# A two-block transformer kernel: first attention normalised on GpSimd, packed gate unit, bias and fill banks reassigned

## Chip, cores and metric

The kernel runs on one core of a Trainium2 chip, as one program. The metric is the device time of one execution in microseconds (us). Engines are named as in the profile: PE is TensorE's matmul side, PEld its weight loads, DVE is VectorE, ACT ScalarE, POOL GpSimd, SP SyncE.

## What is computed

A sequence of 512 tokens with 1024 features goes through two blocks.

- Block one: RMS norm, one wide projection, then three kinds of attention over 8 query heads in 2 groups (compressed keys, selected key blocks, window), each multiplied by a sigmoid gate and added up; beside it a convolution branch (31 taps, 512 channels). With 512 tokens, 8 selection blocks and 16 to be chosen, the selection takes every block, and the window of 512 takes every earlier key. Then a merge, an output projection and a convolutional feed-forward net of width 2816.
- Block two: an even layer with a dense grouped attention and a latent attention (8 heads each, 512 keys), an odd layer with windowed attention of 16 heads with a sink, and a last RMS norm.

The part that the change touches most, from the reference:

```python
p_s = jax.nn.softmax(jnp.where(dist_s >= 0, s_s, NEG_INF), axis=-1)
o_s = jnp.einsum('bgjtm,bgtmd->btgjd', p_s.astype(vsg.dtype), vsg)
...
p_w = jax.nn.softmax(jnp.where(valid_w, s_w, NEG_INF), axis=-1)
o_w = jnp.einsum('bgjts,bsgd->btgjd', p_w.astype(vw.dtype), vw)
...
g = jax.nn.sigmoid(gate_logits).reshape(b, s, G, J, 3)
o = g[..., 0:1] * o_c + g[..., 1:2] * o_s + g[..., 2:3] * o_w
```

## The kernel before

Everything is kept transposed, features on the 128 partitions and 512 tokens along the free dimension. The weights come as 171 units of 128 output features by 1024 input features, in the fixed order of UNITS. SP loads a unit into one of five raw buffers as soon as the PE has finished the unit five places earlier (`unit_done`). POOL splits it: `whi` is the weight rounded to fp32r (L1076, L1077), `wlo` the rest (two halves, L1071); `w_hi` counts units whose first part is made, `w_split` finished ones. The input is split in the same way, so that a unit on the PE (`unit`, L478) is 8 chunks of three 128x512 matmuls: high by high, low by high, high by low; the matmuls of a unit accumulate in one PSUM bank. Each engine's program is written out by hand; where attention steps and units share the PE, the loops below interleave them.

**Banks.** There are eight PSUM banks of 128x512. `Banks.take(pe, pool, key)` gives the next bank of a pool (a tuple of bank numbers) in turn, and makes the PE wait until the last user of that bank was read (`freed`). Turns are counted by the tuple, so that two pools written as the same tuple share a turn: EOUT_REST, E_BANKS and O_BANKS are all (3, 0, 1, 2). TR, for sums and spreads, is (4, 5).

**First attention ("N", L576 to L621).** 32 steps, 4 head pairs by 2 branches (selected, window) by 4 query tiles; step s has qt+1 key tiles. In iteration i the PE does `n_scores(i)` (L585), `n_turn(i-2)` (the probabilities turned, L595), two chunks of a gate unit `ga` or `gb` (L478) and `n_values(i-3)` (L607). DVE adds the bias and takes the maximum (`n_max`, L1958), ACT does the exponential with its row sum (L1329) and copies the turned tile (L1338). The probabilities are not normalised: for each pair p of head and branch DVE takes the reciprocal of 8 row sums and multiplies by the gate (L1967, L1969), the PE spreads the result over the partitions (`n_spread`, L619, 16 rows of the trace), ACT copies that (L1346), DVE multiplies the values bank by it (L1976), adds the branches (L1980) and the compressed branch (L1984). Between these, DVE works through 75 of the convolution's taps (L1832, one 128x512 multiply-add each, both inputs in SBUF), a number per iteration by TAPS_AT. POOL only splits weights in this stage.

**Raw units ("e" and "o", `raw_units`).** The first three units of block two's layers use the input before its norm. The DVE scales their banks afterwards and adds a correction, a 128x2 matmul pair per chunk (`bias`, L495), summed in banks of its own: BIAS_BANK, here bank 3 for the first two units and bank 4 for the third. Of the layer "e", `spread("e")` (L566) lies in bank 4 as well, and is read until the last of eight `h_split` multiplications (L1749), which make the normed input for the fourth unit, `ekr`. In layer "o" the fourth unit `oq3` takes its bank from O_BANKS; `low` (L2407) frees the banks of the raw units oq0, oq1, oq2 one after another once the input is normed.

**Second attention ("AB").** 32 steps; iteration i: scores (L879, L886), turn (L900), `key_prep` (L925, banks C_R), `ab_values(i-3)` (L913), `query_prep` (L930), half a gate unit in bank 0. DVE frees the banks of the preparations. POOL normalises these probabilities (`normalize`: a power -1 of two row sums, L1111, and one multiplication for each half, L1115). **Third attention ("C")**: the same with windows; its values (L1020) always accumulate in bank 6, which `c_out` (L2446) frees after `gates`.

**Start.** Four `conv` units run on unnormed input, high parts first (L658, a wait for `w_split`), then the low parts (L666).

**Gates.** Unit ("tok", 2) has 24 used output rows, the gate logits; it is turned by four transposes.

Of the kernel before, what the change touches and what calls it, by code (L numbers as in the profile page):

```python
# [21 lines left out]
P = 128  # L22
T = 512
# [68 lines left out]
OOUT_BANKS, OOUT_REST = (0, 3, 7), (1, 2, 0, 3)  # L92
# [27 lines left out]
RAW_BANKS, BIAS_BANK = (0, 1, 2), ((3,), (4,))  # L120
# [70 lines left out]
AB_FILL_BANK, AB_S, AB_O = (0,), (1, 2), (3, 6)  # L191
C_FILL, C_S, C_T, C_O, C_R = (3, 0), (1, 2), (4, 5), (6,), (7,)


def program(nc, d, out, known):
    found = {}
    ctx = ExitStack()
    with ctx:
# [80 lines left out]
        nspread = area(T)  # L279
# [94 lines left out]
        def pt_c(p, half, kt, at, n):  # L374

            start = ((p % 2 * 2 + half) * TT + kt) * 3 * P + at * P
            return pt3[:, start:start + n * P]
        sel2, minus1 = sb("sel2", [2]), sb("minus1", [2])
        table = sb("table", [2 * len(ROOTS)])
# [74 lines left out]
        def _(pe):  # L454
# [34 lines left out]
            def bias(tag, layer, j, k, s):  # L489

                if k == 0:
                    bank.take(pe, BIAS_BANK[j // 2], (tag, "bias", j))
                b = bank.tiles[BIAS_BANK[j // 2][0]]
# [5 lines left out]
            def raw_units(tag, layer, units, src, sums_, spread_):  # L499
# [14 lines left out]
                unit(*units[2], src=src, pool=RAW_BANKS, extra=lambda k, s: bias(tag, layer, 2, k, s))  # L514

# [83 lines left out]
            def n_values(s):  # L599
                i, br, qt = n_steps[s]  # L600
                pe.wait_ge(*ptc.at(("N", s, 1)))
                if qt == 0:
                    bank.take(pe, N_O, ("O", "N", s // TT))
                b = bank.tiles[found[("bank", ("O", "N", s // TT))]]
                for kt in range(qt + 1):
                    for half in range(2):
                        m = mm(b[64 * half:64 * half + 64, qt * P:(qt + 1) * P],  # L607
                               vtok[:, kt, br * P + half * HD:br * P + half * HD + HD],
                               npt[:, s % 2, half, kt * P:(kt + 1) * P], start=(kt == 0), stop=(kt == qt),
                               skip_group_check=True)  # L610
                m.then_inc(*pv_done.up(("N", s)))

            def n_spread(p):
                pe.wait_ge(*dve_did.at(("N", "rinv", p)))
                b = bank.take(pe, C_R, ("N", "R", p))
                for qt in range(TT):
                    for half in range(2):
                        x = n_col(p, half, qt)
                        m = mm(b[64 * half:64 * half + 64, qt * P:(qt + 1) * P],  # L619
                               rinv[:, x:x + 1].to_broadcast([P, HD]), ident[:, :], start=True, stop=True)  # L620
                m.then_inc(*pe_did.up(("N", "R", p)))  # L621
# [28 lines left out]
            for i in range(CONV_FIRST):  # L650
                u = UNIT[("conv", i)]
                pe.wait_ge(w_split.sem, u + 1)
                b = bank.take(pe, CONV_BANKS, ("conv", i))
                for k in range(DC):
                    if i == 0:
                        pe.wait_ge(*act_did.at(("n1", "rhi", k)))
                    for w in (whi, wlo):
                        mm(b[:, :], w[:, u % WS, k * P:(k + 1) * P], raw_n(k)[0],  # L658
                           start=(k == 0 and w is whi), stop=False)
# [37 lines left out]
            for i in range(3):  # L697
                unit("tok", i)
# [4 lines left out]
            for i in range(4):  # L703
                unit("q", i, pool=Q_BANKS)
                if i == 0:
                    turn_unit("tok", 2, tokbuf(2))
# [3 lines left out]
            for i in range(n + 4):  # L710
# [14 lines left out]
                if i >= 6 and (i - 6) % TT == 0:  # L725
                    n_spread((i - 6) // TT)
# [136 lines left out]
            unit("ega", 1, pool=E_BANKS)  # L863
            unit("ega", 2, pool=E_BANKS)
# [58 lines left out]
            def key_prep(j):  # L923
                b = bank.take(pe, C_R, ("KN", j))
# [16 lines left out]
            for i in range(n + 4):  # L941
# [8 lines left out]
                if 3 <= i < n + 3:  # L950
                    ab_values(i - 3)
# [4 lines left out]
                if i < 2 * len(AB_FILL):  # L956
                    if i % 2 == 0:
                        part = unit(*AB_FILL[i // 2], inline=False, pool=AB_FILL_BANK)
                    for k in range(4):
                        part(i % 2 * 4 + k)  # L960
                for j, k0, k1 in EOUT_FIRST.get(i, ()):
# [42 lines left out]
            def c_values(i):  # L1004
# [9 lines left out]
                b = bank.tiles[C_O[0]]  # L1014
# [40 lines left out]
        def _(pool):  # L1055
# [10 lines left out]
                            pattern=[[-1, P]], channel_multiplier=1).then_inc(*pool_did.up("const"))  # L1066

# [40 lines left out]
            def normalize(name, s, x, probs):  # L1108
# [1496 lines left out]
```

## Time and profile before

| | |
|---|---|
| runs, us | 1337.38, 1344.39, 1339.45; median 1339.45 |
| profiled execution, us | 1342.96; its span 1341.2 |
| mean granted TensorE clock | 0.982 |
| busy in the span | PE 1298.4, PEld 1027.0, DVE 782.6, ACT 445.6, POOL 818.2 |

Busy time is the union of an engine's instructions. Matmuls overlap in the pipeline: a 128x512 matmul lasts 0.39 in its row, but one starts every 0.23, so time on the PE is read from starts, or from the chain of waits, where a piece is as long as it moves the chain on. An interval after an instruction, in square brackets, is idle time before it and what ended it.

### The profile page before, as it was taken

The page shows a single profiled execution, that of the slowest core. Times are in us where ns is not written, and L with a number is a line of the kernel's source. Part 1 is how long each engine was busy: PE and PEld are TensorE (multiplying, and loading weights), DVE is VectorE, ACT ScalarE, POOL GpSimd, SP SyncE. Part 2 cuts the span into 40 slices and gives each one's busy share as a digit, 9 for nine tenths or more (in the row PEclk, how much of TensorE's full clock was granted, in tenths as well). Part 3 has the DMA queues.
Part 4 walks back from the last instruction along what each step waited for, and adds up shares of the span by engine and source line. Part 5 has one row for each costly group of instructions (what it writes and reads, how often), then busy time and mean ns, then how long its engine had stood idle before and what let it go on. Part 6 is the DMA issues. An engine that isn't in the chain of part 4 may idle for free.

```text
span 1341.2 us, 19796 instructions
## 1 busy us (share of the span) xinstructions
PE 1298.4 (97%) x7118; PEld 1027.0 (77%) x7118; DVE 782.6 (58%) x1512; ACT 445.6 (33%) x947; POOL 818.2 (61%) x916
## 2 busy tenths in 40 slices
PE   7999999999999999999999979999999998999996
PEld 5898767788888888888888868877567786866675
DVE  4897888914654777777652455463655362055532
ACT  5201556513121211222110341245767331145521
POOL 5885322446676766667697463665745464678842
PEclk9999999989999999999999979999999998999998
DMA  4622111122353455555653123221000221311111
GB/s 177 233 80 79 32 40 41 33 64 82 100 180 112 164 199 198 190 188 190 203 171 95 50 91 134 79 64 48 1 1 1 79 85 63 95 47 49 32 48 63
DMA packets 37524, 130.21 MB, mean 97 GB/s; under 512 B 4544, under 2 KB 4928, under 8 KB 37184
## 3 DMA queue, kind: packets, MB, share of 16 engines
q1 hardware_dynamic: 26640, 93.07, 22.0%
q10 hardware_dynamic: 10800, 35.98, 7.2%
q8 instruction: 57, 0.93, 0.3%
q14 instruction: 27, 0.22, 0.1%
HBM read 126.94 MB, written 2.10 MB: 96 GB/s over the span
## 4 chain that ended last, share of the span: by engine, by line
PE 89%; issue 4%; POOL 4%; DVE 1%; ACT 1%; DMA 0%; POOLq 0%; DVEq 0%; ACTq 0%; SPq 0%
PE bank L478 52%; PE bank L777 9%; PE bank L755 3%; POOL wlo L1071 3%; PE bank L913 2%; PE bank L900 2%; PE bank L607 2%; PE bank L585 2%; PE bank L595 2%; PE bank L1020 2%; PE bank L990 2%; PE bank L658 1%; PE bank L886 1%; PE bank L891 1%; PE bank L681 1%
## 5 line engine op out<-in xcount | busy, mean ns | idle before, releaser
L1071 POOL TENSOR_TENSOR wlo<-raw,whi 128x512 fp32r<-128x512 f32 x342 | 466.8, 1385 | 31.1 <-ACT whi L1612 18.1
L478 PE MATMUL bank<-ysplit,whi 128*128 128x512 f32 x984 | 315.5, 399 | 0.2 <-DVE xbuf L2388 0.2
L1076 POOL TENSOR_TENSOR whi<-raw,ones 128x2 fp32r<-128x2 f32 x155 | 40.5, 261 | 373.4 <-DMA raw<-in_w 373.0
L478 PE MATMUL bank<-hhi,whi 128*128 128x512 f32 x536 | 219.8, 410 | 6.1 <-issue 5.5
L478 PEld LDWEIGHTS bank<-ysplit,whi 128*128 128x128 f32 x984 | 183.9, 190 | 39.0 <-issue 3.9
L478 PE MATMUL bank<-hhi,wlo 128*128 128x512 f32 x536 | 211.2, 394 | 0.0
L478 PE MATMUL bank<-hlo,whi 128*128 128x512 f32 x536 | 210.9, 393 | 0.0
L478 PE MATMUL bank<-ysplit,wlo 128*128 128x512 f32 x496 | 194.7, 393 | 0.0
L1077 POOL TENSOR_SCALAR whi<-raw 128x1022 fp32r<-128x1022 f32 x155 | 170.8, 1102 | 0.0
L478 PEld LDWEIGHTS bank<-hhi,whi 128*128 128x128 f32 x536 | 102.1, 190 | 31.8 <-issue 12.3
L478 PEld LDWEIGHTS bank<-hhi,wlo 128*128 128x128 f32 x536 | 101.8, 190 | 22.5
L478 PEld LDWEIGHTS bank<-hlo,whi 128*128 128x128 f32 x536 | 102.2, 191 | 18.4
L478 PEld LDWEIGHTS bank<-ysplit,wlo 128*128 128x128 f32 x496 | 94.1, 190 | 20.1
L1832 DVE SCALAR_TENSOR_TENSOR arena<-first,arena 128x512 f32<-128x512 f32 x120 | 106.6, 938 | 0.2
L1111 POOL TENSOR_TENSOR rinv<-rsum,minus 128x2 f32<-128x2 f32 x64 | 46.2, 722 | 86.2 <-ACT arena L1551 66.8
L1437 ACT ACTIVATE arena<-bank,cols 128x512 f32<-128x512 f32 x44 | 34.4, 781 | 177.7 <-DVE bank L2153 177.7
L1115 POOL TENSOR_SCALAR arena<-arena,rinv 128x512 f32<-128x512 f32 (+2 forms) x128 | 78.1, 624 | 6.3
L2315 DVE CUSTOM_DVE_ANT_0 arena<-bank,arena 128x512 f32<-128x512 f32 x64 | 44.2, 690 | 53.4 <-PE bank L891 34.0
L777 PE MATMUL bank<-hhi,whi 128*128 128x512 f32 x176 | 68.5, 389 | 0.0
L777 PE MATMUL bank<-hlo,whi 128*128 128x512 f32 x176 | 68.5, 389 | 0.0
L777 PE MATMUL bank<-hhi,wlo 128*128 128x512 f32 x176 | 68.5, 389 | 0.0
L2153 DVE TENSOR_TENSOR bank<-bank,arena 128x512 f32<-128x512 f32 x44 | 30.7, 698 | 50.4 <-PE bank L478 50.4
(318 smaller groups left out, 2156.2 us busy)
## 6 DMA issues: line engine op xcount, KB each, us to landing
raw<-in_w SPq DMA_DIRECT2D x171, 512.0 KB, 3.6
arena<-in_ada ACTq DMA_DIRECT2D x48, 512.0 KB, 4.3
xbuf<-in_xT ACTq DMA_DIRECT2D x12, 256.0 KB, 5.2
xbuf<-in_w ACTq DMA_DIRECT2D x1, 2048.0 KB, 10.7
first<-in_w ACTq DMA_DIRECT2D x1, 2048.0 KB, 8.9
out_t<-xbuf SPq DMA_DIRECT2D x8, 256.0 KB, 2.3
xbuf<-in_xT SPq DMA_DIRECT2D x4, 256.0 KB, 6.6
first<-in_uq ACTq DMA_DIRECT2D x1, 768.0 KB, 6.9
```

The source lines that it names most:

```text
L478: m = mm(b[:, :], w[:, s, k * P:(k + 1) * P], x, start=(k == 0 and part == 0), stop=(k == DC - 1 and part == 2))
L755: m = mm(b[:, :], w[:, u % WS, kk * P:(kk + 1) * P], x, start=(k == 0 and part == 0), stop=(k == 3 and part == 2))
L777: m = mm(b[:, :], w[:, u % WS, n * P:(n + 1) * P], x, start=(i == 0 and part == 0), stop=(i == FC - 1 and part == 2))
L1071: return g.tensor_tensor(wlo[:, s, at], raw[:, s, at], whi[:, s, at].bitcast(F32), ALU.subtract)
L1076: g.tensor_tensor(whi[:, s, 0:2], raw[:, s, 0:2], ones[:, :], ALU.mult)
L1077: g.tensor_scalar(whi[:, s, 2:D], raw[:, s, 2:D], 1.0, 1.0, ALU.mult, ALU.mult)\
L1111: g.tensor_tensor(rinv[:, x:x + 2], rsum[:, x:x + 2], minus1[:, :], ALU.pow)\
L1115: g.tensor_scalar(probs(half), probs(half), rinv[:, x + half:x + half + 1], 1.0, ALU.mult, ALU.mult)\
L1437: A(ua[:, i % 4, :], bank.of(("up", i))[:, :], ACT.Identity, scale=col("ffw", order_up(i) * 3 + 2), bias=col("ffb", order_up(i)))\
L1832: V.scalar_tensor_tensor(cacc[:, c, :], z[:, c, k:k + T], w, cacc[:, c, :], ALU.mult, ALU.add)\
L2153: V.tensor_tensor(b[:, :], b[:, :], spread2, ALU.mult).then_inc(*dve_did.up(("un", i)))
L2315: link(V.tensor_tensor_reduce(abp[:, s % 3, half, :], bank.of(("S", "AB", s, half))[:, :], zero, 1.0, -3.0e38, ALU.add, ALU.max, nmax[:, x ...
```

## The change

1. `gate_unit` replaces the unit ("tok", 2): POOL copies the 24 low columns beside the 24 high ones (`whi` columns 32 to 55), so that two matmuls per chunk do for three; `turn_gates` adds the two groups by a matmul with `sum24`.
2. The first attention's probabilities are normalised and gated on POOL (`n_norm`); the PE's `n_turn` waits for that. `n_spread`, its copy and DVE's part go. Both branches of a head pair accumulate in one bank, and `n_out` is one addition. POOL's splits in the stage are cut in three parts, between the normalisations.
3. The first `conv` unit starts when `whi` is there, and does all its high weights first. ACT runs a small Copy before its first real one.
4. BIAS_BANK is bank 3 alone; the third unit's bias goes into the bank of the layer's sums ("fe", "sum") or ("o", "sum"), read and freed earlier.
5. ega1 and ega2 take banks 0 and 3 by pools of their own; fills and preparations of the second attention take banks 0 and 7 in turn, and stand ahead of `ab_values`. E_BANKS' turn is two shorter, so that oq3 falls on bank 0 and not on 2.
6. The third attention's values alternate between banks 6 and 7, OOUT_BANKS ends in 6, and `c_out` stands ahead of `gates`.

```diff
-OOUT_BANKS, OOUT_REST = (0, 3, 7), (1, 2, 0, 3)
+OOUT_BANKS, OOUT_REST = (0, 3, 6), (1, 2, 0, 3)
-RAW_BANKS, BIAS_BANK = (0, 1, 2), ((3,), (4,))
+RAW_BANKS, BIAS_BANK, SUM_OF = (0, 1, 2), (3,), {"e": "fe", "o": "o"}
-AB_FILL_BANK, AB_S, AB_O = (0,), (1, 2), (3, 6)
-C_FILL, C_S, C_T, C_O, C_R = (3, 0), (1, 2), (4, 5), (6,), (7,)
+AB_FILL_BANK, AB_S, AB_O = (0, 7), (1, 2), (3, 6)
+C_FILL, C_S, C_T, C_O, C_R = (3, 0), (1, 2), (4, 5), (6, 7), (7,)
...
                 if k == 0:
-                    bank.take(pe, BIAS_BANK[j // 2], (tag, "bias", j))
+                    pool = BIAS_BANK if j < 2 else (found[("bank", (SUM_OF[tag], "sum"))],)
+                    bank.take(pe, pool, (tag, "bias", j))
...
+            def gate_unit():
+                u = UNIT[("tok", 2)]
+                pe.wait_ge(w_split.sem, u + 1)
+                b = bank.take(pe, WIDE, ("tok", 2))
+                for k in range(DC):
+                    for part, x in enumerate(h_parts(k)):
+                        m = mm(b[:, :], whi[:, u % WS, k * P:(k + 1) * P], x,
+                               start=(k == 0 and part == 0), stop=(k == DC - 1 and part == 1))
+                m.then_inc(*unit_done.up(u))
...
                 for half in range(2):
-                    pe.wait_ge(*p_ready.at(("N", s, half)))
+                    pe.wait_ge(*p_norm.at(("N", s, half)))
...
-                if i >= 6 and (i - 6) % TT == 0:
-                    n_spread((i - 6) // TT)
...
-            unit("ega", 1, pool=E_BANKS)
-            unit("ega", 2, pool=E_BANKS)
+            unit("ega", 1, pool=AB_FILL_BANK[:1])
+            unit("ega", 2, pool=AB_O[:1])
...
-                b = bank.take(pe, C_R, ("KN", j))
+                b = bank.take(pe, AB_FILL_BANK, ("KN", j))
...
+            def n_norm(s):
+                i, b, qt = n_steps[s]
+                normalize("N", s, n_col(s // TT, 0, qt), lambda half: np_[:, s % 3, half, 0:(qt + 1) * P],
+                          lambda half: gate3[:, qt, 3 * (i + 4 * half) + 1 + b:3 * (i + 4 * half) + 2 + b])
...
+            for i in range(len(n_steps)):
+                n_norm(i)
+                if i % TT:
+                    split_part(first + i // TT, i % TT - 1)
...
+            def n_out(i):
+                dve.wait_ge(*act_did.at(("cmp", "o", i)))
+                dve.wait_ge(*pv_done.at(("N", 8 * i + 7)))
+                V.tensor_tensor(nacc(i), bank.of(("O", "N", i))[:, :], ncmp(i), ALU.add)\
+                    .then_inc(*dve_did.up(("N", "o", i)))
```

How the order changes, at two places. On the PE in the first attention, end of iteration 6 and start of iteration 7, before (L607 values, L619 the spread, L585 scores, L595 the turn, L638 and L630 turn and scores of the compressed branch):

```order
L607 MATMUL bank<-arena 64x128 x8
L619 MATMUL bank<-ident,rinv 64x128 x8
L585 MATMUL bank<-split_r 128x512 x6
L595 MATMUL bank<-ident,arena 128x128 x4
L638 MATMUL bank<-ident,arena 128x128 x2
L630 MATMUL bank<-split_r 128x64 x12
```

The same place now (the functions stand on other lines: L628 values, L606 scores, L616 the turn, L649 and L641 the compressed branch):

```order
L628 MATMUL bank<-arena 64x128 x8
L606 MATMUL bank<-split_r 128x512 x6
L616 MATMUL bank<-ident,arena 128x128 x4
L649 MATMUL bank<-ident,arena 128x128 x2
L641 MATMUL bank<-split_r 128x64 x12
```

The spread is gone from the PE, and nothing stands in its place. On POOL, the first two steps and a half of that attention now (before, only rows like the first three stand here, one group per unit; L1130 is the power, L1134 the multiplications, L1119, L1120 and L1090 the parts of a split):

```order
L1095 TENSOR_TENSOR whi<-raw,ones 128x2
L1096 TENSOR_SCALAR whi<-raw 128x1022
L1090 TENSOR_TENSOR wlo<-raw,whi 128x512 x2
L1130 TENSOR_TENSOR rinv<-rsum,minus 128x2
L1134 TENSOR_SCALAR arena<-arena,rinv 128x128 x2
L1130 TENSOR_TENSOR rinv<-rsum,minus 128x2
L1134 TENSOR_SCALAR arena<-arena,rinv 128x256 x2
L1119 TENSOR_TENSOR whi<-raw,ones 128x2
L1120 TENSOR_SCALAR whi<-raw 128x1022
L1130 TENSOR_TENSOR rinv<-rsum,minus 128x2
L1134 TENSOR_SCALAR arena<-arena,rinv 128x384 x2
L1090 TENSOR_TENSOR wlo<-raw,whi 128x512
```

Each step now has a power and two multiplications on POOL, and a unit's split is spread over three steps.

## Rows read from the trace of the kernel before

**Rows 1.** Waits of the PE, whole span: releaser, us in total, times, longest.

```profile
PE bank L658 <- POOL wlo L1071: 9.7, 1, 9.7
PE bank L495 <- DVE bank L1749: 8.4, 1, 8.4
PE bank L478 <- issue: 5.5, 1, 5.5
...
PE bank L1020 <- DVE arena L2446: 1.4, 1, 1.4
```

**Rows 2.** Timeline around the raw units of layer e: start, us, instruction, idle before.

```profile
785.18 0.17 DVE L1692 SCALAR_TENSOR_TENSOR stat<-bank,stat 128x8 f32<-128x8 f32 x1
...
795.84 0.39 PE L478 MATMUL bank<-ysplit,wlo 128*128 128x512 f32 x1
...
804.53 1.60 DVE L1760 SCALAR_TENSOR_TENSOR hlo<-bank,modc,hhi 128x512 fp32r<-128x512 f32 x2
...
804.67 0.37 PE L495 MATMUL bank<-shr,whi 128*128 128x2 f32 x1 [8.45 <-DVE bank L1749]
...
813.51 0.48 PE L478 MATMUL bank<-hhi,whi 128*128 128x512 f32 x1
```

**Rows 3.** Chain of waits in the same unit, one chunk: start, length, what.

```profile
810.79 0.12 PE bank L495 x2
810.90 0.80 PE bank L478 x3
```

**Rows 4.** Busy by window: PE, PEld, DVE, ACT, POOL, granted clock, DMA.

```profile
804.67:809.48 4.81, 4.80 (x15) 4.09 (x16) 1.35 (x2) 0.67 (x1) 0.00 (x0) 0.51 0.00 0
```

**Rows 5.** Timeline, DVE, before the fourth unit of layer o.

```profile
1112.09 2.09 DVE L2407 SCALAR_TENSOR_TENSOR ysplit<-bank,cols,ysplit 128x512 fp32r<-128x512 f32 x3
```

**Rows 6.** Groups with shapes apart, 149 to 271: busy us, mean ns.

```profile
L1832 DVE SCALAR_TENSOR_TENSOR arena<-first,arena 128x512 f32<-128x512 f32 x75 | 64.0, 901 | 0.0
...
L619 PE MATMUL bank<-ident,rinv 128*64 128x128 f32 x128 | 8.3, 273 | 0.0
...
L1976 DVE TENSOR_TENSOR first<-bank,arena 128x512 f32<-128x512 f32 x4 | 2.7, 682 | 0.0
```

**Rows 7.** Busy by window, first attention: all of it, then its later part.

```profile
135.45:261.90 126.45, 124.81 (x997) 91.53 (x996) 112.62 (x263) 74.54 (x220) 40.83 (x34) 1.00 0.11 35
...
217.03:261.90 44.87, 44.87 (x380) 33.52 (x378) 44.13 (x95) 28.04 (x84) 15.59 (x12) 1.00 0.12 37
```

**Rows 8.** Taps while POOL is idle, groups of DVE in 175.5 to 186.5.

```profile
L1832 DVE SCALAR_TENSOR_TENSOR arena<-first,arena 128x512 f32<-128x512 f32 x9 | 6.3, 745 | 0.0
```

**Rows 9.** Timeline: a split's high part amid taps.

```profile
151.79 1.56 POOL L1077 TENSOR_SCALAR whi<-raw 128x1022 fp32r<-128x1022 f32 x1
```

**Rows 10.** POOL's groups, whole span, with shapes apart.

```profile
L1077 POOL TENSOR_SCALAR whi<-raw 128x1022 fp32r<-128x1022 f32 x155 | 170.8, 1102 | 0.0
L1111 POOL TENSOR_TENSOR rinv<-rsum,minus 128x2 f32<-128x2 f32 x64 | 46.2, 722 | 86.2 <-ACT arena L1551 66.8 <-ACT arena L1644 19.3
L1115 POOL TENSOR_SCALAR arena<-arena,rinv 128x512 f32<-128x512 f32 x64 | 44.7, 713 | 3.2
...
L1115 POOL TENSOR_SCALAR arena<-arena,rinv 128x256 f32<-128x256 f32 x32 | 15.0, 482 | 1.6
```

**Rows 11.** Timeline, step 22: the exponential's end and the turn that follows it.

```profile
228.63 0.18 ACT L1329 ACTIVATION_READ_ACCUMULATOR arena<-arena,nmax 128x1 f32 x1
...
232.18 0.87 PE L595 MATMUL bank<-ident,arena 128*128 128x128 f32 x6
```

**Rows 12.** Timeline, start: the fourth unit's split, and the low parts' first matmul.

```profile
20.27 2.57 POOL L1071 TENSOR_TENSOR wlo<-raw,whi 128x512 fp32r<-128x512 f32 x2
...
26.68 1.07 PE L666 MATMUL bank<-split_r,whi 128*128 128x512 f32 x4
```

**Rows 13.** Chain of waits, the unit of the gates.

```profile
106.57 5.50 PE bank L478 x24
```

**Rows 14.** Timeline, second attention: a preparation that waits.

```profile
950.60 1.12 PE L925 MATMUL bank<-arena,first 128*128 128x512 f32 x2 [1.85 <-DVE hhi L2337]
```

More of the change, by code:

```diff
@@ L514, in raw_units, with turn_gates @@
                 unit(*units[2], src=src, pool=RAW_BANKS, extra=lambda k, s: bias(tag, layer, 2, k, s))
+            def gate_unit():
[7 more added lines that the diff above has]
+                m.then_inc(*unit_done.up(u))
+            def turn_gates():
+                pe.wait_ge(*pool_did.at("sum24"))
+                pe.wait_ge(*act_did.at(("tok", 2, "copy")))
+                b = bank.take(pe, TR, ("tok", 2, "T"))
+                for tt in range(TT):
+                    m = mm(b[:, tt * P:tt * P + 24], tokbuf(2)[0:64, tt * P:(tt + 1) * P], sum24[0:64, :], start=True, stop=True)
+                m.then_inc(*pe_did.up(("tok", 2, "T")))
             def turn_unit(name, i, src):
@@ L601, in n_values @@
                 pe.wait_ge(*ptc.at(("N", s, 1)))
-                if qt == 0:
-                    bank.take(pe, N_O, ("O", "N", s // TT))
-                b = bank.tiles[found[("bank", ("O", "N", s // TT))]]
+                if qt == 0 and br == 0:
+                    bank.take(pe, N_O, ("O", "N", i))
+                b = bank.tiles[found[("bank", ("O", "N", i))]]
                 for kt in range(qt + 1):
@@ L608, in n_values @@
                                vtok[:, kt, br * P + half * HD:br * P + half * HD + HD],
-                               npt[:, s % 2, half, kt * P:(kt + 1) * P], start=(kt == 0), stop=(kt == qt),
+                               npt[:, s % 2, half, kt * P:(kt + 1) * P], start=(br == 0 and qt == 0 and kt == 0), stop=(br == 1 and kt == qt),
                                skip_group_check=True)
                 m.then_inc(*pv_done.up(("N", s)))
[L613 to L621, printed above, removed]
             def cmp_scores(qt):
@@ L697, in _ @@
             for i in range(3):
-                unit("tok", i)
+                if i < 2:
+                    unit("tok", i)
+                else:
+                    gate_unit()
                 if i == 0:
@@ L1106, in split_part, with normalize @@
                     m.then_inc(w_split.sem, 1)
-            def normalize(name, s, x, probs):
+            def normalize(name, s, x, probs, gate=lambda half: 1.0):
                 pool.wait_ge(*p_ready.at((name, s, 1)))
@@ L1246, in _ @@
                 act.dma_start(xT[:, c, :], d["xT"][c]).then_inc(*xload[c].up(0, 16))
+            act.wait_ge(*pool_did.at("ones"))
+            A(table[:, 2 * len(ROOTS):], ones[:, :], ACT.Copy).then_inc(*act_did.up("first table"))
             act.wait_ge(*n1g_load.at("n1g"))
@@ L1340, in n_copy @@
                     bank.freed(("T", "N", s, half), ptc, ("N", s, half))
-            def n_spread_copy(p):
-                act.wait_ge(*pe_did.at(("N", "R", p)))
-                if p:
-                    act.wait_ge(*dve_did.at(("N", "t", p - 1)))
-                A(nspread, bank.of(("N", "R", p))[:, :], ACT.Copy).then_inc(*act_did.up(("N", "R", p)))
-                bank.freed(("N", "R", p), act_did, ("N", "R", p))
             def cmp_exp(qt):
```

83 lines of the change are left out of this document (40 added, 43 removed).

## The prediction

> **What bounds the kernel now.** I read the busy shares first: the PE is busy for 1298.4 of 1341.2 us, so a microsecond counts only if it leaves the PE's work or one of its gaps. Then its waits [rows 1]: apart from 9.7 us at the start, they are 8.4 and 5.5 us in the raw units of the second block's two layers, and single ones under 2 us. Third, stretch by stretch, who is close behind the PE: in the first attention it is DVE, busy for 112.6 of 126.5 us, and for 44.1 of the last 44.9 [rows 7]. There the PE alone does not set the pace.
>
> The sum is made against the profiled execution, 1342.96 us, which lies 3.5 above the median of the runs, 1339.45.
>
> **The raw units of layer e (-10.0).** The PE ends its second raw unit at about 796.2 (the last matmul: 795.84 and 0.39) and then waits 8.45 us at the bias matmul of the third [rows 2]. The bias wants bank 4, which held `spread("e")`; the last L1749 reads it until 804.6. In the change it takes the bank of the sums, last read at 785.35, when L1692 ends [rows 2]. The weights are no limit, since the PE had waited for nothing else. So the unit can start at 796.2. The wait costs a second time now: the granted clock is 0.51 for the 4.81 us after it, thus 1.2 GHz [rows 4], and at 2.4 GHz a chunk takes 0.80+0.12 = 0.92 [rows 3]. The unit ends at 796.2+8x0.92 = 803.6, where it ended at 813.5 [rows 2]: 9.9 us. What is late next is the normed input of `ekr`: the last two of its eight chunks are ready at 806.1 [rows 2], and `ekr` comes to its last one at 803.6+7x0.69 = 808.4. So no new wait. DVE's scaling of the third unit follows at 806.1, the sums that need it come after `ekr` and another unit. Bounds: 8.45 if the clock stays low anyway, 10.5 if all is better. I take 10.0.
>
> **Layer o (-1.4).** `oq3` waited for the third of three L2407, 2.09 us together [rows 5]; on bank 0 it waits for the first. That saves 2x0.70. The rest of the 5.5 us [rows 1] stays, since all three come after the normed input. Bounds 1.0 and 2.0.
>
> **Gates (-1.8).** A unit of 24 matmuls takes 5.50, 0.229 each [rows 13]; 8 go. The four small matmuls in place of the transposes I take as equal. POOL's copy of 192 numbers per partition comes long before the unit is wanted. Bounds 1.5 and 2.0.
>
> **Second and third attention (-2.6).** The second `key_prep` waited 1.85 us for DVE [rows 14], in a bank that it now doesn't need; `query_prep`, 1.12 later, does need what DVE frees then, so 0.7 of the wait goes there: -1.1. Double fill banks take away a smaller wait at its start, -0.2. In the third, the values' wait of 1.4 for `c_out` [rows 1] goes with the second bank: -1.3. Bounds of the group: 0 and 3.5.
>
> **Start (0).** The first unit can start some 2 us earlier. But the first four are paced by POOL: the fourth's split ends at 22.84, and its 16 matmuls of 0.23 end at 26.5, where the low parts start now at 26.68 [rows 12]. The PE would wait for the second split in place of the first. Bounds: 0.3 gained, 1 lost by gaps at the low clock. The extra Copy on ACT is hidden in the same wait.
>
> **The first attention (-4, the open term).** From the PE go 8 spreads, 8.3 us of busy time in the group, and nothing comes for it [rows 6]. That is the upper bound, -8.2. Against it stands what POOL gets: 32 powers of 0.72 = 23.1 us, and 64 multiplications of 0.71, 0.60, 0.48 and, extended down, 0.37 for the four widths, 34.6 [rows 10]; 57.7 beside 40.8 busy now, in a stage of 126.5 [rows 7]. POOL has the room. But its instructions and the taps get in each other's way: a tap takes 0.745 while POOL is idle [rows 8] and 0.901 over the stage [rows 6], so 75 taps lose 11.7 us to 40.8 us of POOL, 0.29 per us. The high part of a split, one SBUF input like the multiplications, takes 1.56 amid taps [rows 9], against 1.10 on average [rows 10].
>
> DVE over the stage: 112.6 now. It loses seven of eight multiplications L1976 of 0.68, three of its adds, and the short reciprocals, about 10.5; it gains 0.29x57.7 = 16.7 if the power counts like the others, 0.29x34.6 = 10.0 if it doesn't. So DVE comes to 112 to 119 against a PE of 126.5-7.1 = 119.4. In the last third: 44.1, less 4.2, plus 12.9x0.29 = 3.7 or 21.6x0.29 = 6.3, gives 43.6 to 46.2, against a PE of 44.9-3.1 = 41.8. So the last third gains nothing, the rest some 3 of its 4.1, the spread after the loop its 1.0: -4. The other bound is all of POOL's added time landing on DVE: 102.1+57.7 = 159.8, 33 us more than now.
>
> The Trainium skill has a rule that speaks against this edit (SBUF — State Buffer, "Who interferes with whom"): the port pair that DVE and GpSimd share is an exclusive lock, and a DVE instruction with two SBUF inputs and a GpSimd instruction that reads SBUF block each other for a whole instruction. By it every multiplication that falls among taps costs DVE its full length, and the term would be near zero or a loss. The trace agrees with blocking as far as it goes: 1.56 is the average 1.10 and more than half a tap.
>
> The added wait itself: `n_turn(i-2)` stands ahead of the fill and the values on the PE, and ACT's copies and DVE's maxima wait behind it. The shortest time from an exponential's end to its turn is about that of step 22, 228.81 to 232.18, 3.4 us [rows 11]. POOL needs 0.72+0.60 for the first half, and up to 1.6 more if it is in half a split. That fits, narrowly.
>
> **Sum.** -10.0-1.4-1.8-2.6-4.0 = -19.8: 1342.96-19.8 = 1323.2, or from the median **1319.6**; I say 1320.
>
> **Rivals.**
> - *The ports eat the whole of the first attention's gain* or a little more (0 to +4 there). For it: DVE at 44.1 of 44.9, and the blocked split. Against: the taps are 64.0 of DVE's 112.6 us, the rest of its work is mostly on PSUM, and before 217 us it has 13 us idle (81.6 less 68.5) [rows 6, 7]. Time: 1339.45-15.8+2 = 1326. Chance 0.22. The Trainium skill's rule on the port pair would lead here.
> - *The bank was not what the third raw unit waited for*: the same 8.4 us come back at `ekr` or in the weights, by then 10 us sooner wanted. Against it: the normed chunks at 806.1 and a wait put down to L1749, the last reader of that bank. Time 1319.6+10 = 1330. Chance 0.06.
> - *Slower: POOL and DVE lock each other in the first attention*, so that the PE waits at each step for the normalised probabilities or the maxima. To outweigh the other 15.8 us the stage must lengthen to 142.3, that is DVE by 40.2 of POOL's added 57.7, 70% of it landing on taps; today it is 29%. With all of it the time is 1339.45-15.8+33.4 = 1357; in the middle of that stretch 1348. Chance 0.04.
> - *The edit does less than it says elsewhere* (waits move one place on in every stage, first attention as forecast): 1335. Chance 0.03.
> - The forecast, within a few us: 0.65.
>
> **Numbers.** A measurement of this kernel can tell 0.5%, 6.7 us, from no change. The forecast, the first rival and the second lie below 1332.7: faster 0.93; the last one (0.03) and a mild case of the lock (0.01) give same 0.04; the rest of the lock is slower 0.03. The range reaches down to the full 8.2 us of the spreads and the upper bounds elsewhere, -26 with the spread of the runs, 1312, and up to the first rival and part of the second, 1329.
>
> **What would show it.** No PE wait at the third raw unit's bias and the clock at full speed from there through `ekr`; a shorter wait at `oq3`, ended by the first L2407; the gate unit at 3.7. In the first attention: taps longer than 0.90 on average, DVE at 95% or more, PE gaps of a few tenths before scores and turns, and the stage 3 to 5 us shorter in all. I am wrong if the PE waits there by whole microseconds, if the stage shortens by the full 8, or if the raw units' wait stands again behind them.

## The result, and the profile after

| | before | after |
|---|---|---|
| median, us (runs) | 1341.87 (6) | 1329.54 (6) |
| lowest to highest | 1337.38 to 1344.39 | 1323.86 to 1332.28 |
| profiled execution, its span | 1342.96, 1341.2 | 1329.59, 1327.8 |
| busy: PE, DVE, POOL | 1298.4, 782.6, 818.2 | 1290.1, 775.5, 890.9 |

The ratio is 0.991, 95% interval 0.9883 to 0.9937. The kernel is faster, but by 12 us where the forecast was 20: 1329.54 lies just above the range of 1312 to 1329. The forecast of 1320 started from 1339.45, the median of three executions; six give 1341.87, so 2.4 of the 9.5 us between 1320 and 1329.54 lie in where it started and not in the change.

I laid both traces beside each other at points that both programs pass on the PE. The table gives by how much each stretch of the profiled execution became longer (+) or shorter (-); the last column is the forecast's term.

| stretch, by its first matmuls | us | forecast |
|---|---|---|
| start, to the low parts | +0.1 | 0 |
| to the first attention (the gate unit is in it) | -1.1 | -1.8 |
| first attention, to the down projection | +4.9 | -4 |
| block two to `ekr`'s end (raw units of layer e) | -10.9 | -10.0 |
| second attention | -3.8 | -1.3 |
| layer o | -1.1 | -1.4 |
| third attention | -1.5 | -1.3 |
| sum | -13.4 | -19.8 |

One term has the wrong sign. By itself it is 8.9 us off, more than the whole miss of 6.4 here; the other terms together came out 2.5 better than forecast. These are the PE's waits now (releaser, us in total, times, longest), to be read against [rows 1]:

```profile
PE bank L674 <- ACT split_r L1264: 8.2, 1, 8.2
PE bank L616 <- POOL arena L1134: 6.3, 7, 2.3
PE bank L478 <- issue: 4.2, 1, 4.2
...
PE bank L606 <- DVE nmax L1993: 1.8, 2, 1.2
```

The 8.4 us at the bias are gone, the wait at `oq3` is 1.3 shorter, the 1.4 at the third attention's values is gone. New is the second line: the turn (`n_turn`, now L616) waits for POOL's multiplications. Busy by window in the first attention (PE, PEld, DVE, ACT, POOL, granted clock, DMA), whole, from 217, and the 3.4 us behind the longest of these waits:

```profile
134.45:274.80 140.35, 130.33 (x948) 92.54 (x947) 114.40 (x246) 72.36 (x216) 119.49 (x134) 0.99 0.12 35
...
217.00:274.80 57.80, 51.23 (x376) 35.90 (x375) 44.36 (x83) 26.13 (x77) 54.59 (x55) 0.97 0.10 30
...
267.50:270.90 3.40, 3.40 (x13) 2.75 (x12) 0.00 (x0) 1.20 (x2) 3.32 (x5) 0.50 0.01 2
```

The stage took 134.5 us before (135.45 to 269.98) and takes 140.35. Where DVE was the engine close behind the PE [rows 7], it now has slack, 44.4 of 57.8; POOL has 54.6 of 57.8, where it had 15.6 of 44.9. The chain of waits from 216 to 267 us runs over POOL alone, with nothing between its instructions but 0.1 us of issue per step. Its last part (start, length, what):

```profile
245.27 1.25 POOL wlo L1090
246.52 1.12 POOL rinv L1130
...
247.73 2.56 POOL arena L1134 x2
250.29 1.69 POOL wlo L1090
251.98 1.12 POOL rinv L1130
...
253.19 0.88 POOL arena L1134 x2
254.07 0.67 POOL rinv L1130
...
254.84 2.03 POOL arena L1134 x2
256.86 0.59 POOL whi L1119
257.45 1.02 POOL whi L1120
258.48 0.68 POOL rinv L1130
...
259.25 3.14 POOL arena L1134 x2
```

Two multiplications of 384 columns take 3.14 us at 259.25, two of 512 columns 2.56 at 247.73. The groups of the stage (busy, mean ns, idle before) show that the powers and the multiplications are longer than I had costed them:

```profile
L1867 DVE SCALAR_TENSOR_TENSOR arena<-first,arena 128x512 f32<-128x512 f32 x78 | 67.9, 917 | 0.0
...
L1130 POOL TENSOR_TENSOR rinv<-rsum,minus 128x2 f32<-128x2 f32 x32 | 28.6, 893 | 15.6 <-ACT arena L1373 14.9 <-DVE arena L1867 0.6
...
L1134 POOL TENSOR_SCALAR arena<-arena,rinv 128x512 f32<-128x512 f32 x16 | 16.6, 1043 | 0.8
...
L1134 POOL TENSOR_SCALAR arena<-arena,rinv 128x384 f32<-128x384 f32 x16 | 14.0, 886 | 0.8
...
L1134 POOL TENSOR_SCALAR arena<-arena,rinv 128x256 f32<-128x256 f32 x16 | 12.6, 796 | 0.8
```

I had costed the power at 0.72 and the multiplications at 0.71, 0.60 and 0.48, by [rows 10]. The taps went from 0.901 to 0.917 only [rows 6]. So what the new instructions lose came out of POOL, not out of DVE: the 96 of them take 28.6 + 52.7 = 81.3 us, where the forecast had 57.7. (POOL's whole 119.5 us can't be held against 40.8 + 57.7: the 40.8 leave out the last 8 us of the stage. Over the whole of it the splits kept POOL busy for 46.1 us before and for 38.2 now, 38 instructions each time.) From an exponential's end to the end of its second multiplication it took 1.9 us at step 0, 4.9 at step 21 and 7.7 at step 31.

### The profile page after: what moved, and what is told of

Read it like the earlier page. It is cut to its first block, busy times and chain, and to the rows that moved or that the text cites. A ratio compares the mean times of both kernels' runs of the same rounds, so it can differ in the third digit from the quotient of the medians.

```text
span 1327.8 us, 19481 instructions
## 1 busy us (share of the span) xinstructions
PE 1290.1 (97%) x6986; PEld 1018.0 (77%) x6986; DVE 775.5 (58%) x1484; ACT 440.7 (33%) x940; POOL 890.9 (67%) x1014
## 4 chain that ended last, share of the span: by engine, by line
PE 85%; POOL 8%; issue 4%; DVE 2%; DMA 1%; ACT 1%; POOLq 0%; SPq 0%; ACTq 0%; DVEq 0%
PE bank L478 50%; PE bank L794 9%; PE bank L772 3%; POOL wlo L1090 3%; PE bank L930 2%; PE bank L917 2%; POOL arena L1134 2%; PE bank L1007 2%; PE bank L1037 2%; PE bank L674 1%; PE bank L908 1%; PE bank L903 1%; PE bank L697 1%; PE bank L1017 1%; PE bank L896 1%
## 5 line engine op out<-in xcount | busy, mean ns | idle before, releaser
L1090 POOL TENSOR_TENSOR wlo<-raw,whi 128x512 fp32r<-128x512 f32 x342 | 460.5, 1365 | 30.4 <-ACT whi L1647 18.1
L478 PE MATMUL bank<-hhi,whi 128*128 128x512 f32 x528 | 216.9, 411 | 4.5 <-issue 4.2
L1095 POOL TENSOR_TENSOR whi<-raw,ones 128x2 fp32r<-128x2 f32 x146 | 36.9, 253 | 274.3 <-DMA raw<-in_w 274.1
L478 PEld LDWEIGHTS bank<-ysplit,whi 128*128 128x128 f32 x984 | 183.2, 189 | 38.2 <-issue 3.2
L478 PE MATMUL bank<-hhi,wlo 128*128 128x512 f32 x528 | 208.3, 394 | 0.0
L1096 POOL TENSOR_SCALAR whi<-raw 128x1022 fp32r<-128x1022 f32 x146 | 159.7, 1094 | 0.0
L1130 POOL TENSOR_TENSOR rinv<-rsum,minus 128x2 f32<-128x2 f32 x96 | 74.8, 779 | 96.4 <-ACT arena L1586 62.6
L1134 POOL TENSOR_SCALAR arena<-arena,rinv 128x384 f32<-128x384 f32 (+3 forms) x192 | 131.1, 694 | 9.7
L478 PEld LDWEIGHTS bank<-hhi,whi 128*128 128x128 f32 x528 | 101.1, 191 | 28.6 <-issue 9.3
L1867 DVE SCALAR_TENSOR_TENSOR arena<-first,arena 128x512 f32<-128x512 f32 x120 | 110.2, 968 | 0.2
L794 PE MATMUL bank<-hhi,whi 128*128 128x512 f32 x176 | 68.5, 389 | 0.0
L794 PE MATMUL bank<-hhi,wlo 128*128 128x512 f32 x176 | 68.5, 389 | 0.0
```

What stands on the lines that cost most here:

```text
L478: m = mm(b[:, :], w[:, s, k * P:(k + 1) * P], x, start=(k == 0 and part == 0), stop=(k == DC - 1 and part == 2))
L794: m = mm(b[:, :], w[:, u % WS, n * P:(n + 1) * P], x, start=(i == 0 and part == 0), stop=(i == FC - 1 and part == 2))
L1090: return g.tensor_tensor(wlo[:, s, at], raw[:, s, at], whi[:, s, at].bitcast(F32), ALU.subtract)
L1095: g.tensor_tensor(whi[:, s, 0:2], raw[:, s, 0:2], ones[:, :], ALU.mult)
L1096: g.tensor_scalar(whi[:, s, 2:D], raw[:, s, 2:D], 1.0, 1.0, ALU.mult, ALU.mult)\
L1130: g.tensor_tensor(rinv[:, x:x + 2], rsum[:, x:x + 2], minus1[:, :], ALU.pow)\
```

## Experiments

Three theories stand against each other. **Ports**: taps and POOL's instructions exclude each other, POOL loses, and in the last third it is the bound. **Own work**: POOL would be late even undisturbed, by the number and length of what it was given. **DVE**: DVE holds the stage, and POOL's lateness follows. The first runs' "theory POOL" says only that POOL is late, and leaves open which of the first two makes it so. Several runs were made on other chips, where the kernel before has medians of its own (1339.35, 1342.95 and 1340.06); the ratios are against those.

### Each part by itself

First attention as before, all else as changed:

```diff
-                    pe.wait_ge(*p_norm.at(("N", s, half)))
+                    pe.wait_ge(*p_ready.at(("N", s, half)))
...
+                if i >= 6 and (i - 6) % TT == 0:
+                    n_spread((i - 6) // TT)
```

> The changed kernel with the first attention as before (spreads on the PE, POOL only splitting) and all other parts of the change kept. In the changed kernel's trace that stage lasts 140.35 us where it lasted 134.53, 5.8 more. Theory POOL (GpSimd is the bound of that stage's last third): the stage comes back to 134.5, the PE's waits on POOL's multiplications and the low clock at 267.5 to 270.9 are gone, and the kernel takes 1329.5 - 5.8 = 1323.7. Rival (the other parts cost here too, by banks or by the earlier start): the stage stays above 136 and the kernel above 1326.

Measured 1321.49 (1321.21 to 1322.81), ratio 0.987 (0.9846 to 0.9893). All its runs are below all of the changed kernel's. The stage is 134.63 us again, and POOL idle for two thirds of it:

```profile
134.12:268.75 134.63, 132.93 (x1063) 97.70 (x1064) 119.76 (x272) 76.26 (x223) 46.22 (x38) 1.00 0.12 36
```

The profiled execution is 7.3 us shorter than the changed kernel's, 5.7 of it in this stage, the rest in pieces of 0.3 to 0.7 at the start, the merge and the second attention. The POOL theory's number, 1323.7, is met and bettered by 2.

The third bias alone, on the kernel before:

```diff
-                    bank.take(pe, BIAS_BANK[j // 2], (tag, "bias", j))
+                    pool = BIAS_BANK if j < 2 else (found[("bank", (SUM_OF[tag], "sum"))],)
+                    bank.take(pe, pool, (tag, "bias", j))
```

> The kernel before with the third bias alone moved to the bank of the sums. The sum of the prediction says -10.0 (8.45 of wait, the rest the clock); the changed kernel's trace shows that stretch 10.9 shorter, so 1341.9 - 10.9 = 1331.0. Rival (part of the 10.9 came from elsewhere, or the wait comes back at ekr): 1334 or more.

Measured 1330.93 (1322.72 to 1332.71), ratio 0.9929 (0.9902 to 0.9955). In its trace the stretch from the raw units to `ekr`'s end is 10.9 us shorter than before. The wait did not come back: its largest waits are the start and `oq3`. The stretch of the trace shows this better than the times, which are 8.4 us apart by the medians of one chip (1339.35 before) and 12.5 by the profiled executions.

```profile
PE bank L659 <- POOL wlo L1072: 9.8, 1, 9.8
PE bank L478 <- issue: 5.5, 1, 5.5
PE bank L991 <- DVE nmax L2426: 2.0, 7, 0.3
```

The first attention's part alone, on the kernel before (the reverse of the first edit):

> The kernel before with the first attention's part of the change alone. Theory POOL: slower by the 5.8 us of the stage, 1341.9 + 5.8 = 1347.7, with the PE waiting some 6 us on POOL's multiplications after 217 us. Rival (it costs only together with the other parts): 1342 or less.

Measured 1347.12 (1342.31 to 1351.55), ratio 1.0058 (1.0039 to 1.0078): this part of the change, alone, makes the kernel slower. The median is 7.8 above that of before; the profiled execution is 4.0 longer, with 4.7 in the stage where I had expected 5.8. Its waits:

```profile
PE bank L594 <- POOL arena L1102: 4.7, 7, 1.0
PE bank L977 <- DVE nmax L2396: 2.0, 7, 0.3
PE bank L584 <- DVE nmax L1948: 1.9, 2, 1.2
```

### Less work for POOL

DVE takes the reciprocal, POOL has no powers:

```diff
-                normalize("N", s, n_col(s // TT, 0, qt), ...
+                pool.wait_ge(*dve_did.at(("N", "rinv", s)))
...
+            def n_recip(s):
+                x = n_col(s // TT, 0, n_steps[s][2])
+                dve.wait_ge(*p_ready.at(("N", s, 1)))
+                V.reciprocal(rinv[:, x:x + 2], rsum[:, x:x + 2]).then_inc(*dve_did.up(("N", "rinv", s)))
```

> The changed kernel, but the reciprocal of the row sums is taken by DVE (32 instructions of 2 columns, 0.2 us each at most by the row of 8 columns, 6 us) in place of POOL's 32 powers (28.6 us there). Theory POOL: POOL has 119.5 - 28.6 = 91 us left in a stage of 134, it is no longer back to back after 214 us, the waits of 6.3 us and the low clock (1.5) go: 1329.5 - 8 = 1321.5 or a little more for the additional DVE time. Rival DVE (the stage is held by DVE, with 114.4 us busy, and POOL's lateness only follows): DVE gets 6 us more, and the kernel takes 1330 to 1336. Rival order (half a split stands in the way of each multiplication): the waits stay at half their size, 1326.

Measured 1329.65 (1323.99 to 1332.62), ratio 0.9919 (0.989 to 0.9947): no gain. This was the surprise. The stage takes 142.36 us, and the PE waits for POOL for 8.3 us at 13 places. The powers' 28.6 us are gone, and POOL's multiplications took most of them back:

```profile
L1143 POOL TENSOR_SCALAR arena<-arena,rinv 128x512 f32<-128x512 f32 x16 | 23.3, 1461 | 5.5 <-DVE rinv L2006 5.5
L1143 POOL TENSOR_SCALAR arena<-arena,rinv 128x256 f32<-128x256 f32 x16 | 20.0, 1260 | 23.7 <-DVE rinv L2006 23.7
L1143 POOL TENSOR_SCALAR arena<-arena,rinv 128x384 f32<-128x384 f32 x16 | 16.8, 1058 | 0.8 <-DVE rinv L2006 0.3
L1143 POOL TENSOR_SCALAR arena<-arena,rinv 128x128 f32<-128x128 f32 x16 | 13.3, 838 | 1.8 <-DVE rinv L2006 1.8
```

Together 73.4 us, against 52.7. Here POOL is released by DVE's reciprocal, and DVE's next instructions are the taps, so that the pairs of multiplications run into them: of the 32 pairs, 22 begin while a tap is in progress, where it is 10 in the changed kernel. POOL also stands idle for 31 us, waiting for the reciprocals. The POOL theory in its simple form (take work from POOL and it will be in time) fell here. The DVE theory's number, 1330 to 1336, is nearly met, but by chance at most: DVE is busy for only 111.7 us of 142.4. What remained was to vary the taps and the multiplications one at a time.

### The taps out of the way

Taps of iteration 18 and later for 8 columns (the convolution is left incomplete):

```diff
-                V.scalar_tensor_tensor(cacc[:, c, :], z[:, c, k:k + T], w, cacc[:, c, :], ALU.mult, ALU.add)\
+                V.scalar_tensor_tensor(cacc[:, c, 0:N], z[:, c, k:k + N], w, cacc[:, c, 0:N], ALU.mult, ALU.add)\
...
-                    taps(TAPS_AT[i] if i < len(TAPS_AT) else len(steps))
+                    taps(TAPS_AT[i] if i < len(TAPS_AT) else len(steps), T if i < 18 else 8)
```

> The changed kernel with each convolution tap of the first attention from iteration 18 on done for 8 of its 512 columns (same instructions and waits; the convolution's output is left incomplete). Theory ports (the taps block POOL's multiplications, powers and splits: a multiplication of 512 columns is 0.77 us undisturbed and 1.04 on average, up to 1.88): after 210 us every multiplication is 0.45 to 0.77 and every power 0.70, POOL falls from 54.6 us in the last 57.8 to 43 or less and is no longer back to back, and the waits for it end; the stage gives back at least the 8.4 us that its last third lost, 1329.5 - 8 or more = 1321 or less. Rival own work (POOL would be late even undisturbed): it stays back to back after 214 us, and at least half of the 6.3 us of waits stays: 1325 or more.

Measured 1318.26 (1317.33 to 1318.32), ratio 0.9813 (0.9795 to 0.9831); one of its four executions took 4413 us and is left out. The stage takes 130.4 us, 10 less than in the changed kernel, and no wait for POOL is left. POOL's groups in the last 51.5 us of the stage:

```profile
L1130 POOL TENSOR_TENSOR rinv<-rsum,minus 128x2 f32<-128x2 f32 x13 | 9.2, 705 | 6.0 <-ACT arena L1373 5.6
L1134 POOL TENSOR_SCALAR arena<-arena,rinv 128x512 f32<-128x512 f32 x8 | 6.4, 805 | 0.4
L1134 POOL TENSOR_SCALAR arena<-arena,rinv 128x384 f32<-128x384 f32 x6 | 3.9, 661 | 0.3
...
L1134 POOL TENSOR_SCALAR arena<-arena,rinv 128x256 f32<-128x256 f32 x6 | 3.3, 555 | 0.3
```

In the changed kernel the same four stand at 921, 1190, 1171 and 1198 ns there, all three widths at the same mean; only the 128-wide ones are no longer than here (535 against 598). So undisturbed POOL is in time, and waits for exponentials for 6 us: own work, with the same instructions in the same order, is not the cause. (DVE's time shrinks in this run too; but DVE was not what the PE waited for after 217.)

### The multiplications out of the way

Only 8 columns of each tile are normalised, the rest stays unnormalised; DVE keeps all its taps:

```diff
-lambda half: np_[:, s % 3, half, 0:(qt + 1) * P],
+lambda half: np_[:, s % 3, half, 0:8],
```

> The changed kernel with only the first 8 columns of each probability tile normalised on POOL in the first attention (64 multiplications short, the powers and splits kept; the rest of the tile goes on unnormalised). Theory ports: POOL loses some 45 of its 119.5 us, no wait for it remains, the taps come back from 0.917 towards 0.90, and the stage takes 134.5 - 7 = 127.5, that is 1329.5 - 13 = 1316.5; what is missing of that is what DVE costs when POOL is out of the way. Rival DVE (the stage is bound by DVE in its last third as before): no more than 1323.

Measured 1319.62 (1313.49 to 1320.57), ratio 0.9827 (0.9812 to 0.9842). The stage is 130.7 us, 9.6 less than in the changed kernel though DVE does all it did, so DVE is not what held it; the waits for POOL go from 6.3 to 1.7. It is not the 127.5 that I had expected: POOL lost 19 us of multiplications, not 45, for this is what the short ones take:

```profile
L1134 POOL TENSOR_SCALAR arena<-arena,rinv 128x8 f32<-128x8 f32 x64 | 33.8, 540 | 3.3
```

The timeline of four pairs, the second without a tap beside it, the others with one, two and more:

```profile
219.43 1.21 POOL L1134 TENSOR_SCALAR arena<-arena,rinv 128x8 f32<-128x8 f32 x2
...
221.40 0.68 POOL L1134 TENSOR_SCALAR arena<-arena,rinv 128x8 f32<-128x8 f32 x2
...
228.80 1.98 POOL L1134 TENSOR_SCALAR arena<-arena,rinv 128x8 f32<-128x8 f32 x2
...
256.19 4.03 POOL L1134 TENSOR_SCALAR arena<-arena,rinv 128x8 f32<-128x8 f32 x2
```

At 221.40 DVE works on PSUM (L1993), at the others it is in taps. Of the 64, 48 took 0.34 or 0.35 us each, and none of these shared more than 0.07 us with a tap; the 16 that met a tap took 0.85 to 2.04, 1.1 on average. What a POOL instruction pays is not a share of its length: it stands still until a tap has ended, and at 256.19 each of the two stands still through about three taps that follow each other without a gap. The Trainium skill (SBUF — State Buffer, "SBUF: two separate sides") says that of a DVE instruction with two SBUF inputs and a GpSimd one that reads SBUF, the one that starts first gets the shared port pair for the whole instruction and the other fully blocks. The trace agrees, with 0.34 against 1.1 for the same eight columns.

It works the other way too. In the changed kernel, these are three taps beside the half of a split that POOL began at 230.04, where three undisturbed ones take 2.1 us:

```profile
229.66 3.31 DVE L1867 SCALAR_TENSOR_TENSOR arena<-first,arena 128x512 f32<-128x512 f32 x3
```

Of the stage's 78 taps, 15 take 1.0 us or more, up to 1.82: ten stood behind a part of a split and five behind a multiplication. In the kernel before it was 13 already, all behind splits, so that the change added little to DVE's loss.

### Taps moved to where DVE is idle

```diff
-TAPS_AT = (1, 1, 1, 1, 4, 1, 3, 1, 2, 1, 3, 2, 3, 3, 3, 2, 3, 2, 3, 1, 3, 2, 3, 2, 3, 3, 3, 1, 3, 2, 3, 2, 2, 2)
+TAPS_AT = (2, 2, 2, 2, 4, 1, 3, 1, 2, 1, 3, 2, 3, 3, 3, 3, 3, 3, 3, 1, 2, 2, 2, 2, 2, 3, 2, 1, 2, 2, 2, 2, 2, 2)
```

> The changed kernel with six taps moved from iterations 20 to 30 of the first attention to iterations 0 to 3, 15 and 17, where DVE has idle time; nothing is left out. Theory ports: in the last third each tap that is gone gives POOL back up to half of it, and DVE all of it: about 6 x 0.5 = 3 us of POOL's chain, 1329.5 - 3 = 1326.5. Rival own work (POOL late whatever DVE does): 1329.5. Rival early waits (the taps make the maxima late at the start): 1330 or more.

Measured 1328.49 (1327.39 to 1330.2), ratio 0.9909 (0.9889 to 0.9929): the same as the changed kernel, for two reasons that cancel.

```profile
PE bank L616 <- POOL arena L1134: 3.6, 3, 2.8
PE bank L606 <- DVE nmax L1993: 3.3, 2, 2.0
...
156.20:163.00 6.80, 6.67 (x30) 5.66 (x32) 4.64 (x14) 2.25 (x7) 4.30 (x7) 0.50 0.00 0
```

Between 218 and 264 us, iteration by iteration, the PE gains 4.3 us as the ports theory has it, and of the seven waits for POOL three stay. In the first iterations the maxima come later (waits of 1.2 and 2.0), and the clock falls to half for 6.8 us behind the longer one; by iteration 9 the PE is 4.7 us behind the changed kernel. Both the ports and the early-waits theory named something real; the total does not tell them apart, the trace does.

### The second attention

```diff
                 if i in PREP_K:
                     key_prep(PREP_K[i])
+                if 3 <= i < n + 3:
+                    ab_values(i - 3)
                 if i in PREP_Q:
...
-                if 3 <= i < n + 3:
-                    ab_values(i - 3)
```

> The changed kernel with the second attention's values at their old place, ahead of query_prep and the fill. The changed kernel's stage is 3.8 us shorter than before where I had forecast 1.3; by function on the PE the turns took 34.2 us and take 30.3, because a turn followed by a fill moves on after 0.87 us and one followed by the values after 1.02. Theory order: +2.8, 1329.5 + 2.8 = 1332.3. Rival banks (the gain came from the double banks): less than 0.5 us.

Measured 1329.27 (1328.38 to 1329.33), ratio 0.9897 (0.9881 to 0.9912). The order theory's net falls, with 0.7 for its 2.8: the stage is 161.57 us, where the changed kernel's is 160.84, and behind `oq3` a shorter stretch of half clock (3.4 us for 6.8) hides even that in the time. With the old order the stage is 3.1 us shorter than before, and its trace shows where: the first two iterations are 0.9 shorter, since the first fill no longer waits for its bank, and the second `key_prep` has no gap at all and comes 2.1 earlier.

The changed kernel gets its 3.8 in another way. By iteration, each turn with a fill behind it is 0.2 shorter than before, 13 times, 2.6 in all: the order's gain is real, about as large as its theory had it. But the 0.9 at the start are gone, because the second iteration's scores now wait for DVE's maxima, and at the second `key_prep` 1.2 come of the 2.1, because `query_prep` behind it has to wait, where the forecast had put 0.7. The new order gives and takes, and what stays of it is the 0.7. The two waits:

```profile
PE bank L896 <- DVE nmax L2331: 0.6, 1, 0.6
...
939.64 1.02 PE L942 MATMUL bank<-arena,first 128*128 128x512 f32 x2
...
941.54 1.99 PE L947 MATMUL bank<-arena,first 128*128 128x512 f32 x4 [0.87 <-DVE hhi L2353]
```

### A faster version

First attention as before, and `oq3` in bank 3:

```diff
                 unit("oq", i, first=(lambda k: dve_did.at(("o", "h", k))) if i == len(RAW_O) else None,
-                     pool=O_BANKS)
+                     pool=O_BANKS if i > len(RAW_O) else (3,))
```

> The kernel with the first attention as before, and beside it oq3 in bank 3, which nothing else holds by then. In the changed kernel oq3 starts at 1102.1 behind a gap of 4.2 us, and the clock is at half from 1100.4 to 1107.2, worth 3.4. Its normed input is ready at 1097.7 but for two chunks. Theory bank: both go, 1321.5 - 7.6 = 1313.9, or less of it where the next wait is near. Rival input (it waits for the last normed chunks): 1320 to 1321.5.

Measured 1315.15 (1314.95 to 1316.07), ratio 0.9793 (0.978 to 0.9807): 6.3 us below the version before it, of the 7.6 expected. The two were measured on different chips; their profiled executions are 6.2 apart, and the wait and the half clock at this place are gone from the trace. `oq3` starts right behind the last bias, and the clock stays up:

```profile
1090.99 0.17 PE L497 MATMUL bank<-shr,whi 128*128 128x2 f32 x1
...
1091.13 0.48 PE L479 MATMUL bank<-hhi,whi 128*128 128x512 f32 x1
...
1088.00:1100.00 12.00, 12.00 (x58) 10.06 (x57) 9.15 (x15) 4.64 (x7) 7.21 (x7) 1.00 0.30 89
```

On the same, POOL's scheme for the first two head pairs alone, and spreads for the other two:

```diff
-N_FILL, N_S, N_O = (0,), (1, 2), (3, 6)
+N_FILL, N_S, N_O, FUSED = (0,), (1, 2), (3, 6), 16
...
-                    pe.wait_ge(*p_ready.at(("N", s, half)))
+                    pe.wait_ge(*(p_norm if s < FUSED else p_ready).at(("N", s, half)))
...
-                if i >= 6 and (i - 6) % TT == 0:
+                if i >= 6 + FUSED and (i - 6) % TT == 0:
                     n_spread((i - 6) // TT)
```

> The kernel of the last call (first attention as before, oq3 in bank 3) with the first two of four head pairs normalised on POOL and the other two by spreads. In the changed kernel's trace the PE is 1.6 us ahead of the kernel before when step 18's spread would have come (four spreads of 0.87 saved, 1.95 lost to two waits for DVE), and POOL is not yet back to back. Theory (POOL's scheme pays while POOL has idle time): 1315.2 - 1.6 = 1313.6. Rival (what is won there is lost to DVE, which bounds the last third): 1315.2, or up to 1 more.

> The same kernel as x8_best, for the comparison on one chip: 1315.2.

On one chip: 1313.66 (1309.42 to 1316.23) and 1315.81 (1315.42 to 1316.09), ratios 0.9807 (0.9784 to 0.983) and 0.9815 (0.9793 to 0.9836). By time they can't be told apart. The profiled execution, 1309.42, is the fastest of its five, and 3.2 us of its lead come from a shorter half-clock stretch in the raw units of layer e (3.4 us in place of 10.2; see the end of the next section). What belongs to the edit is the stage, 2.5 us shorter (134.55 in the trace of the version without it), with the PE waiting for POOL nowhere:

```profile
134.88:266.95 132.07, 129.57 (x999) 94.25 (x1000) 119.66 (x258) 73.66 (x219) 81.70 (x87) 1.00 0.12 37
```

## Why the prediction was wrong, point by point

- **Direction and most terms: right.** Layer e: 10.9 for 10.0, shown by the experiment that does it alone; the PE has no wait there, and `ekr` met no new one. At 10.9 it is a little above its bound of 10.5: the wait of 8.45 and half of the 4.81 us at half clock [rows 4] make 10.9. Layer o 1.1 for 1.4, third attention 1.5 for 1.3, start 0.1 for 0.
- **The first attention: the step that failed.** "POOL has the room", and "That fits, narrowly". I had seen that a tap and a POOL instruction lengthen each other, and had both numbers (a tap 0.745 or 0.901, a high part 1.10 or 1.56), but charged the loss to DVE alone, 0.29 for each microsecond of POOL, and costed POOL's 96 new instructions at the lengths they have in the second attention, where no taps run. In their place the runs showed: DVE's taps grew by 0.016 each, 1.3 us in all, and the 96 instructions took 81.3 us for the 57.7 that I had put, which left POOL next to no idle time from 214 us on (busy for 51.5 of the 53.5 us to 267.5). The allowance for the turn (0.72 + 0.60 + 1.6 against 3.4) also took each step by itself; a queue that is over-full passes its lateness on, and the last step's was 7.7.
- Of the stage's +5.8 us, by iteration on the PE: the spreads gave 8 x 0.87 = 7.0 (I took 8.2 of busy time as the bound); two waits for DVE at iterations 5 and 9 took 1.95; and everything from iteration 21 on took 10.9. Of these 6.3 are the waits for POOL and 1.7 the low clock (3.4 us at half) behind the 2.3 us wait. The other 2.9 are what remains; the matmuls behind a wait start up to a few tenths late beyond the gap itself, but I did not add these up one by one.
- **The slower rival had the right mechanism and the wrong victim.** I set its point of decision by how much of POOL's time lands on taps (70%). The right measure was on the other side: POOL's own busy share in the last third, 54.6 of 57.8 us. The rival that the ports eat the whole gain gave 1326; of the mechanisms it was nearest, and too mild by 4 in the stage (+2 for +5.8). The rival on the bank gave 1330, the very time, by luck: the wait it spoke of did not come back.
- **Gates: the term was mis-sized.** "The four small matmuls in place of the transposes I take as equal." They are not (chain of waits of the changed kernel):

```profile
106.66 3.69 PE bank L524 x16
...
116.28 1.00 PE bank L534 x8
117.28 5.67 PE bank L478 x24
```

  The unit fell from 5.50 [rows 13] to 3.69 as forecast; but the four matmuls leave 8 rows and take 1.00 where the transposes took 0.44, and the unit behind them 0.17 more. So 1.1 for 1.8.
- **Second attention: mis-sized the other way**, 3.8 for 1.3. The term for the preparations was right: 1.2 for 1.1, with 0.87 of the wait of 1.85 [rows 14] left at `query_prep`. The first fill's 0.2 did not come. What the sum lacked was the 2.6 that the turns gain by having a fill and not the values behind them; no term stood for it.
- Of what I had named as proof of error, one came: the PE waits by a whole microsecond and more in the first attention (2.3 at the most).

Open: why the half-clock stretch of 10.2 us in the raw units of layer e is there in most executions and not in all. In the changed kernel's trace it covers 782.9 to 793.1, with the PE busy throughout; what the PE did just before, from 779.7 on, were 16 matmuls of one column. The run with 8-column multiplications that was profiled has none there, and is 6 us faster than its other runs; the one with two head pairs on POOL has 3.4 us of it. One of six runs of the changed kernel (1323.86, by a mean granted clock of 0.99 in place of 0.984) looks the same, and so do two of the six with the reciprocal on DVE (1323.99 and 1324.26). No run here tests it, and medians of a few executions move with it by some us.

```profile
782.90:793.10 10.20, 10.20 (x38) 9.04 (x37) 1.55 (x9) 1.66 (x3) 9.95 (x11) 0.50 0.15 51
```

## What to carry to other kernels

When two engines exclude each other, charge the loss to both. Here most of it fell on the one that got many short instructions: it stood still once per instruction that met a tap, whatever its size, while the taps, which come in runs, grew by 0.016 us on average. Cost a moved instruction by a row from beside its new neighbours, not from a stage where they are absent, and add up the receiving engine's queue over the tightest third, not over the stage. And where a wait is ended by a bank's last reader, look for a bank that nobody holds before anything else: here two such edits are worth 10.9 and some 6 us, without a new wait on the PE.

## What was unexpected of the hardware

- A GpSimd multiplication of 8 columns takes 0.34 us alone and 0.85 to 2.04 when a DVE instruction with two SBUF inputs is in progress, even with a single SBUF tile as its own input; the 2-column power takes 0.70 alone and up to 1.17.
- It can stand still through more than one: 2.04 us cover about three taps that follow each other without a gap.
- Taking 28.6 us of powers from POOL gained nothing, since its other instructions moved to start while a tap is in progress, 22 pairs of 32 in place of 10: their mean for 512 columns went from 1043 to 1461 ns. When an instruction is released can count for more than what it does.
- Four matmuls of 24 columns in f32 leave eight rows and last 1.00 us, four transposes to 128 columns 0.44.
